# Second mixer of a two-block layer: gate tiles moved amid the last attention pairs, a sigmoid written as a tanh, and an output projection that starts with the state-space half

## The chip, the cores and the metric

The kernel runs on one core of a Trainium2 chip. The metric is the device time of one execution in microseconds (us); lower is better. The engines are PE (TensorE, the matrix engine, with a queue of weight loads of its own), DVE (VectorE), ACT (ScalarE), POOL (GpSimd) and SP (SyncE, which here only issues DMAs). Each runs its own instructions in order and waits on semaphores for the others.

## The reference, cut to what matters

Two blocks run one after the other on x of 512 tokens by 1024 features, all in float32. The change lies in the second block, between the end of its projections and its feed-forward network:

```python
def _s5(u, ...):                      # state-space half, 512 features
    ...                               # scan over time, y
    z = jax.nn.gelu(y.reshape(bsz, seq, D_SSM))
    out = z * jax.nn.sigmoid(z @ w_glu.astype(f32) + b_glu.astype(f32))
    return out.astype(u.dtype)

# second_block
y_ssm  = _s5(u, ...)
y_attn = _swa_sink(q, k, v, rel_bias, sinks[l])   # 8 heads, window of 128, sinks
mixed = jnp.concatenate([_rms(y_ssm, out_norm_ssm[l]),
                         _rms(y_attn, out_norm_attn[l])], axis=-1)
x = x + g1 * (mixed @ w_out[l])                   # 1024 x 1024
h2 = _rms(x, norm2_w[l]) * (1 + sc2) + sh2
x = x + g2 * _conv_ffn(h2, w_up[l], conv_w[l], conv_b[l], w_down[l])
```

## The kernel before

Activations lie transposed: features on the 128 partitions, the 512 tokens along the free axis, in tiles of 128 x 512. Every large product is made in three passes (`split_mm`, lines 133 to 135): weight and activation are each split in a rounded part and a rest, and hi·hi, hi·lo and lo·hi are added up in PSUM. Weights stream in chunks of 128 x 2048 through two buffers. For chunk n, SP loads it (`load_chunk`), ACT makes the rounded part (`round_chunk`, or `next_weights` inside the mixer), DVE the rest (`rest_chunk`, `next_rest`), and PE counts `w_used` up when it has used it, which lets ACT round chunk n + 1.

The second mixer is one block of code. After its projections comes a loop over 16 pairs, p = 0 to 15. A pair is two heads (r = 0, 1) and one chunk of 128 queries. For each pair

- PE makes `scores(p + 2)` and `turn(p)` (the transposes of the probabilities), and after every fourth pair `values(g)`;
- DVE makes `bias(p + 1)` (bias and maximum) and `normalise(p)`;
- ACT makes `exps(p)` and `move(p - 1)` (the transposed probabilities from PSUM to SBUF), and later `store(g)`.

So each pair goes PE, DVE, ACT, DVE, PE, ACT, with buffers for three pairs of probabilities and two banks of scores. Between the pairs, at places written out by hand, stands the rest of the state-space half: `lags(b)` and `from_states(b)` on PE, `output(b)` on ACT and `spin_back` on DVE:

```python
LAGS_AT, STATES_AT, OUTPUT_AT = (2, 5, 8), (3, 6, 10), (1, 4, 7, 11)
SPIN_AT = (1, 3, 5, 7, 9)
```

A second block of code follows when all engines have ended the first. ACT makes four GELUs and rounds them to `zhi`, DVE makes `zlo`, PE makes the gate product (48 matmuls of 128 x 512 into banks 0 to 3, feature by feature), ACT the sigmoid, DVE the product with z. Meanwhile the attention half is squared for its norm `r5`, rounded and split, and PE begins the output projection with it: `out2(c, ...)` is one half of one of four weight chunks, 24 matmuls. The order is attention 0, attention 1, state-space 0, state-space 1, and then attention and state-space in turn. Each norm's sum of squares goes through one float32 matmul with ones (`pe_sum`, line 194) after POOL has added up the squares. DVE scales each result by gate and root, POOL adds the attention part to x, and DVE the state-space part. Then comes the norm `r6` over x (`act_square`, `pe_sum` lines 194 and 197, `act_root`), a table load for SiLU (line 2674), `shifted_act` and `shifted_dve`, and the feed-forward network `ffn2`.

Of the kernel before, what the change touches and what calls it, by code (L numbers as in the profile page):

```python
# [166 lines left out]
class Norm:  # L167


    def __init__(self, k, name, acc, root, bank):  # L170
        self.acc, self.root, self.bank = acc, root, bank
        self.squared, self.added, self.summed, self.rooted, self.inverted, self.rounded, self.split = (
            k.sem(f"{name}_{what}") for what in
            ("squared", "added", "summed", "rooted", "inverted", "rounded", "split"))

    def act_square(self, act, k, src, j):
        if j >= 4:
            act.wait_ge(self.added, max(1, j - 4))
        act.activation(k.sq[:, j % 4, :], src, ACT.Square).then_inc(self.squared, 1)

    def add(self, eng, k, j):

        eng.wait_ge(self.squared, j + 1)
        if j == 1:
            ins = eng.tensor_tensor(self.acc[:, :], k.sq[:, 0, :], k.sq[:, 1, :], ALU.add)
        else:
            eng.wait_ge(self.added, j - 1)
            ins = eng.tensor_tensor(self.acc[:, :], self.acc[:, :], k.sq[:, j % 4, :], ALU.add)
        ins.then_inc(self.added, 1)

    def pe_sum(self, pe, k, added, tail):
# [3 lines left out]
        for j in tail:  # L195
            pe.wait_ge(self.squared, j + 1)
            mm = pe.matmul(self.bank[:, :], k.ones[:, :], k.sq[:, j % 4, :], start=False, stop=j == tail[-1])  # L197
# [425 lines left out]
def program(nc, io):  # L623
    root_ctx = ExitStack()
    with root_ctx:
# [724 lines left out]
        ssm_ctx = ExitStack()  # L1350
        powers = sb("b_powers", [P, TS, 2, 4, P], ctx=ssm_ctx)
# [496 lines left out]
        def _(pe):  # L1848
# [109 lines left out]
            for half in range(2):  # L1958
# [57 lines left out]
        root_a, root_b = k.root, square_sum  # L2016

# [12 lines left out]
        (sm_zhi, sm_zlo, sm_sig, sm_done, v_made, v_turned, v_summed, v_scanned, s_parts, s_made, lag_sum, lag_zero,  # L2030
         lag_set, lag_skip, y_made, y_sum) = (k.sem(f"ssm_{w}") for w in (
             "z_rounded", "z_split", "sigmoid", "done", "inputs", "turned_in", "summed", "scanned", "parts", "states",
# [14 lines left out]
        LAGS_AT, STATES_AT, OUTPUT_AT = (2, 5, 8), (3, 6, 10), (1, 4, 7, 11)  # L2047
        SPIN_AT = (1, 3, 5, 7, 9)
# [68 lines left out]
        def _(pool):  # L2117
            pool.wait_ge(lag_sum, 1)
            pool.memset(lag[:, :, :, :], 0.0).then_inc(lag_zero, 1)
            pool.wait_ge(h3_rounded, KT)  # L2120
            pool.wait_ge(h3_split, KT)
            pool.wait_ge(hot_in, 32)
            nc.clear_and_free_semaphores(feed_sems)

        @block.scalar
        def _(act):
# [95 lines left out]
            for p in range(PAIRS + 1):  # L2222
# [8 lines left out]
                if p == PAIRS - 1:  # L2231
                    act.preload_act_table_set("gelu_apprx_tanh_and_others")
# [4 lines left out]
                if p == 6:  # L2237
                    next_weights(OUT2)
                if p >= NT + 2 and p % NT == 2:
                    store(p // NT - 1)  # L2240
            store(3)
            own.act = chain.n

        @block.vector
        def _(dve):
# [73 lines left out]

            def bias(p):  # L2320
# [28 lines left out]
            chain.link(dve.tensor_scalar(g_heads2[:, 0:4], g_heads2[:, 0:4], HD ** -0.5, None, ALU.mult))  # L2349
            second_tile(IN2, 1)  # L2350
# [33 lines left out]
            for p in range(PAIRS):  # L2384
# [9 lines left out]
                if p == 2:  # L2394
                    next_rest(GLU)
                if p == 8:
                    next_rest(OUT2)
            own.dve = chain.n

        @block.tensor  # L2400
        def _(pe):
# [95 lines left out]

            pe.wait_ge(k.w_lo, IN2 + 1)
# [57 lines left out]
            for p in range(PAIRS):  # L2556
# [19 lines left out]
            values(NT - 1)  # L2576
        stage.close()
        gone(mix_ctx)
        gone(ssm_ctx)


        UP2 = OUT2 + 4
        tail_ctx = ExitStack()
        xhi = nc.alloc_sbuf_tensor_at("xhi_ffn2", [P, KT, S], R, offset=o_at)
        xlo = sb("xlo_ffn2", [P, KT, S], R, tail_ctx)
        hhi = sb("hhi2", [P, HALF, S], R, tail_ctx)
        hlo = sb("hlo2", [P, HALF, S], R, tail_ctx)
        zhi = sb("zhi", [P, 4, S], R, tail_ctx)
        zlo = sb("zlo", [P, 4, S], R, tail_ctx)
        part = sb("out2_part", [P, 4, S], ctx=tail_ctx)  # L2590
        root_a, root_b = sb("root_attn", [P, S], ctx=tail_ctx), sb("root_ssm", [P, S], ctx=tail_ctx)
        sum_b = sb("square_sum_ssm", [P, S], ctx=tail_ctx)
        r5 = Norm(k, "r5", square_sum, root_a, k.bank[6])
        r4 = Norm(k, "r4", sum_b, root_b, k.bank[7])
        r6 = Norm(k, "r6", square_sum, k.root, k.bank[6])
        h6_scaled, h6_rounded, h6_split = k.sem("norm2_scaled"), k.sem("norm2_rounded"), k.sem("norm2_split")
        out_a, part_a, part_b, added_a, added_b, stored = (
            k.sem(f"out2_{w}") for w in ("attn", "attn_scaled", "ssm_scaled", "attn_added", "added",
                                         "stored"))
        ffn2 = FeedForward(k, "ffn2", UP2, io["w_up2"], io["w_down2"], xhi, xlo, hhi, hlo)  # L2600
        o_attn, o_ssm = pr("o_attn"), pr("o_ssm")
        bank_a, bank_b = (4, 0, 6, 2), (2, 4, 0, 4)

        with nc.Block() as block:

            @block.sync
            def _(sp):
                for n in range(OUT2 + 3, ffn2.last):
# [329 lines left out]
```

## Time and profile before

| | us |
|---|---|
| median of 3 runs | 1252.51 |
| their range | 1252.3 to 1253.71 |
| the profiled execution's own time | 1248.42 |
| its span (first to last instruction) | 1246.3 |
| TensorE busy in the span | 1201.6 |
| VectorE busy | 772.5 |
| ScalarE busy | 486.8 |
| GpSimd busy | 62.1 |

The span is what the trace covers; the profiled execution was 2.1 us longer than that and 4.1 us shorter than the median of the runs. Busy time is summed over records; matmuls are pipelined, so a busy PE isn't one at its peak. The granted clock is given as a share of TensorE's 2.4 GHz, and a stretch at 0.50 ran at 1.2 GHz.

### The profile page before, as it was taken

The page shows a single profiled execution, that of the slowest core. Times are in us where ns is not written, and L with a number is a line of the kernel's source. Part 1 is how long each engine was busy: PE and PEld are TensorE (multiplying, and loading weights), DVE is VectorE, ACT ScalarE, POOL GpSimd, SP SyncE. Part 2 cuts the span into 40 slices and gives each one's busy share as a digit, 9 for nine tenths or more (in the row PEclk, how much of TensorE's full clock was granted, in tenths as well). Part 3 has the DMA queues.
Part 4 walks back from the last instruction along what each step waited for, and adds up shares of the span by engine and source line. Part 5 has one row for each costly group of instructions (what it writes and reads, how often), then busy time and mean ns, then how long its engine had stood idle before and what let it go on. Part 6 is the DMA issues. An engine that isn't in the chain of part 4 may idle for free. (4 is left out here: it accounts for less than half of the span.)

```text
span 1246.3 us, 14741 instructions
## 1 busy us (share of the span) xinstructions
PE 1201.6 (96%) x5909; PEld 938.9 (75%) x5909; DVE 772.5 (62%) x1274; ACT 486.8 (39%) x744; POOL 62.1 (5%) x76
## 2 busy tenths in 40 slices
PE   7999998899999999999998999789899999999998
PEld 5786666468778788878886885578688888888887
DVE  6537574756677777775876587656765543455542
ACT  6244545725322212222375234673444421343320
POOL 0000000013100000000022000034000000000000
PEclk9999999999999999999999999999999999999999
DMA  9312121223465576353226531102122223332222
GB/s 355 130 64 68 35 68 34 102 81 128 148 228 193 172 248 248 127 177 116 76 96 170 179 109 35 35 34 102 58 82 97 80 94 114 102 101 101 70 93 91
DMA packets 31884, 144.67 MB, mean 116 GB/s; under 512 B 3303, under 2 KB 9672, under 8 KB 22600
## 3 DMA queue, kind: packets, MB, share of 16 engines
q1 hardware_dynamic: 31816, 143.73, 33.9%
q8 instruction: 47, 0.77, 0.2%
q14 instruction: 21, 0.17, 0.0%
HBM read 136.90 MB, written 6.82 MB: 115 GB/s over the span
## 5 line engine op out<-in xcount | busy, mean ns | idle before, releaser
L133 PE MATMUL bank<-xhi_ffn,w_hi_part 128*128 128x512 f32 x704 | 278.2, 395 | 4.4 <-DVE xlo_ffn L233 4.4
L121 ACT ACTIVATE w_hi_part<-w_raw 128x2048 fp32r<-128x2048 f32 (+1 forms) x95 | 164.1, 1727 | 289.1 <-PE bank L135 287.3
L134 PE MATMUL bank<-xlo_ffn,w_hi_part 128*128 128x512 f32 x704 | 275.7, 392 | 0.0
L135 PE MATMUL bank<-xhi_ffn,w_lo_part 128*128 128x512 f32 x704 | 274.9, 391 | 0.0
L127 DVE TENSOR_TENSOR w_lo_part<-w_raw,w_hi_part 128x2048 fp32r<-128x2048 f32 (+1 forms) x95 | 195.4, 2057 | 94.5 <-ACT w_hi_part L121 91.3
L133 PEld LDWEIGHTS bank<-xhi_ffn,w_hi_part 128*128 128x128 f32 x704 | 132.6, 188 | 35.0 <-issue 6.6
L135 PEld LDWEIGHTS bank<-xhi_ffn,w_lo_part 128*128 128x128 f32 x704 | 132.6, 188 | 30.4
L134 PEld LDWEIGHTS bank<-xlo_ffn,w_hi_part 128*128 128x128 f32 x704 | 132.4, 188 | 28.5 <-issue 0.2
L361 DVE SCALAR_TENSOR_TENSOR squares<-bank,param,squares 128x511 f32<-128x511 f32 x88 | 63.9, 747 | 84.7 <-ACT squares L344 83.1
L133 PE MATMUL bank<-hhi,w_hi_part 128*128 128x512 f32 x240 | 94.6, 394 | 0.3 <-DVE w_lo_part L127 0.3
L133 PE MATMUL bank<-hhi_half,w_hi_part 128*128 128x512 f32 x240 | 94.1, 392 | 0.0
L134 PE MATMUL bank<-hlo,w_hi_part 128*128 128x512 f32 x240 | 93.5, 389 | 0.0
L134 PE MATMUL bank<-hlo_half,w_hi_part 128*128 128x512 f32 x240 | 93.4, 389 | 0.0
L135 PE MATMUL bank<-hhi,w_lo_part 128*128 128x512 f32 x240 | 93.4, 389 | 0.0
L135 PE MATMUL bank<-hhi_half,w_lo_part 128*128 128x512 f32 x240 | 93.4, 389 | 0.0
L448 DVE SCALAR_TENSOR_TENSOR mod_acc<-mod_w,mod_c,mod_acc 128x384 f32<-128x384 f32 x112 | 69.1, 617 | 10.1 <-DMA mod_w<-in_w_mod 6.8
L133 PE MATMUL bank<-xhi,w_hi_part 128*128 128x512 f32 x144 | 61.4, 426 | 7.2 <-DVE w_lo_part L981 7.2
L344 ACT ACTIVATE squares<-bank,param 128x512 f32<-128x512 f32 x44 | 31.9, 776 | 82.8 <-PE bank L135 82.8
L135 PE MATMUL bank<-xhi,w_lo_part 128*128 128x512 f32 x144 | 57.3, 398 | 0.0
L134 PE MATMUL bank<-xlo,w_hi_part 128*128 128x512 f32 x144 | 56.9, 395 | 0.0
L133 PEld LDWEIGHTS bank<-hhi_half,w_hi_part 128*128 128x128 f32 x240 | 45.0, 188 | 12.9 <-issue 2.9
L133 PEld LDWEIGHTS bank<-hhi,w_hi_part 128*128 128x128 f32 x240 | 45.0, 188 | 11.4 <-DVE w_lo_part L127 1.2
(359 smaller groups left out, 1789.8 us busy)
## 6 DMA issues: line engine op xcount, KB each, us to landing
mod_w<-in_w_mod SPq DMA_DIRECT2D x32, 768.0 KB, 4.4
w_raw<-in_w_gu SPq DMA_DIRECT2D x22, 1024.0 KB, 6.4
w_raw<-in_w_down SPq DMA_DIRECT2D x32, 704.0 KB, 4.2
w_raw<-in_w_up SPq DMA_DIRECT2D x22, 1024.0 KB, 4.9
w_raw<-in_w_in_f SPq DMA_DIRECT2D x8, 1024.0 KB, 4.9
w_raw<-in_w_out SPq DMA_DIRECT2D x8, 1024.0 KB, 4.9
w_raw<-in_w_in SPq DMA_DIRECT2D x5, 1024.0 KB, 4.9
x<-in_x SPq DMA_DIRECT2D x8, 256.0 KB, 6.0
```

Of the source, the lines that this page charges most:

```text
L121: act.activation(k.whi[:, slot, 0:width], k.raw[:, slot, 0:width], ACT.Copy).then_inc(k.w_hi, 1)
L127: dve.tensor_tensor(k.wlo[:, slot, 0:width], k.raw[:, slot, 0:width], k.whi[:, slot, 0:width].bitcast(F), ALU.subtract).then_inc(k.w_lo, 1)
L133: pe.matmul(out, whi, xhi, start=first, stop=False)
L134: pe.matmul(out, whi, xlo, start=False, stop=False)
L135: return pe.matmul(out, wlo, xhi, start=False, stop=last)
L344: act.activation(k.sq[:, s, :], k.bank[s][:, :], ACT.Identity, bias=bias[:, 2 * i + a:2 * i + a + 1], scale=taps[:, 6 * i + 3 * a + 2:6 * ...
L361: dve.scalar_tensor_tensor(out=y, in0=k.bank[s][:, 0:S - back], scalar=taps[:, tap:tap + 1], in1=y, op0=ALU.mult, op1=ALU.add).then_inc(se ...
L448: ins = dve.scalar_tensor_tensor(out=acc, in0=w, scalar=self.c[:, j:j + 1], in1=acc, op0=ALU.mult, op1=ALU.add)
```

## The change

What follows is one diff cut to its core; "..." marks what is left out.

- The second block of code is gone: its instructions follow in the first, so the engines don't meet between the two. The buffers are laid over tiles that are free by then.
- The state-space work moves to earlier pairs: the last `from_states` and `output` from pairs 10 and 11 to 7 and 8, the spins to pairs 0 to 4. The split of the gate's weights on DVE moves from pair 2 to pair 6.
- At pair 9 ACT loads the GELU table, makes four GELUs and loads the exp table. `zhi` and `zlo` are made at pairs 10 and 11.
- The gate product goes tile by tile, 12 matmuls each, all in bank 6: `glu(t)` stands ahead of `turn(12 + t)` and, from t = 1 on, waits for `gate_tanh(t - 1)` to have read the bank.
- sigmoid(a) is made as (1 + tanh(a/2))/2: tanh is in the exp table; the factor 1/2 goes into the bias, the gain and the squares; `gate(t)` is one DVE instruction that makes (tanh + 1)·z.
- Rounding, splitting and squaring of the attention half move to pairs 12 and 15 and behind the loop.
- The output projection goes state-space 0, attention 0, state-space 1, and so on in turn. POOL adds the state-space part, DVE the attention part.
- `pe_sum` of r4 and r5 takes two added tiles and one tail tile, which makes two float32 matmuls with ones where it was one.
- POOL clears the semaphores of an earlier block before the memset of the lag weights instead of after it, and DVE scales two small parameters by a half.

```diff
-        LAGS_AT, STATES_AT, OUTPUT_AT = (2, 5, 8), (3, 6, 10), (1, 4, 7, 11)
-        SPIN_AT = (1, 3, 5, 7, 9)
+        LAGS_AT, STATES_AT, OUTPUT_AT = (2, 4, 6), (3, 5, 7), (1, 4, 6, 8)
+        SPIN_AT = (0, 1, 2, 3, 4)
+        GELU_AT, GLU_AT = 9, 12
...
         @block.gpsimd
         def _(pool):
-            pool.wait_ge(lag_sum, 1)
-            pool.memset(lag[:, :, :, :], 0.0).then_inc(lag_zero, 1)
             pool.wait_ge(h3_rounded, KT)
             pool.wait_ge(h3_split, KT)
             pool.wait_ge(hot_in, 32)
+            pool.wait_ge(lag_sum, 1)
             nc.clear_and_free_semaphores(feed_sems)
+            pool.memset(lag[:, :, :, :], 0.0).then_inc(lag_zero, 1)
...
+            def attn_round(g):
+                act.wait_ge(l_stored, g + 1)
+                plain_round(act, r5, ahi[:, g, :], y[:, 4 + g, :], o_attn[:, g:g + 1])
+                r5.act_square(act, k, y[:, 4 + g, :], g)
+
+            def gate_tanh(t):
+                act.wait_ge(sm_made, t + 1)
+                act.activation(tanhs[:, t, :], k.bank[6][:, :], ACT.Tanh, bias=b_half[:, t:t + 1], scale=0.5)\
+                    .then_inc(sm_sig, 1)
+
+            def ssm_round(t):
+                act.wait_ge(sm_done, t + 1)
+                plain_round(act, r4, shi[:, t, :], y[:, t, :], o_half[:, t:t + 1])
...
-                if p == PAIRS - 1:
-                    act.preload_act_table_set("gelu_apprx_tanh_and_others")
                 if p >= 1:
...
-                if p == 6:
+                if p == 7:
...
+                if p == GELU_AT:
+                    act.preload_act_table_set("gelu_apprx_tanh_and_others")
+                    for t in range(4):
+                        act.wait_ge(y_sum, t + 1)
+                        act.activation(y[:, t, :], y[:, t, :], ACT.Gelu_apprx_tanh).then_inc(sm_gelu, 1)
+                    act.preload_act_table_set("exp_and_others")
+                if p in (GELU_AT + 1, GELU_AT + 2):
+                    for t in (0, 1) if p == GELU_AT + 1 else (2, 3):
+                        act.wait_ge(sm_gelu, t + 1)
+                        act.activation(zhi[:, t, :], y[:, t, :], ACT.Copy).then_inc(sm_zhi, 1)
+                if p == GELU_AT + 3:
+                    attn_round(0)
+                    attn_round(1)
+                if p == PAIRS - 1:
+                    attn_round(2)
+                if p > GLU_AT:
+                    gate_tanh(p - GLU_AT - 1)
+                if p > GLU_AT + 1:
+                    ssm_round(p - GLU_AT - 2)
+            ssm_round(3)
+            r4.act_square(act, k, y[:, 0, :], 0, 0.5)
+            r4.act_square(act, k, y[:, 1, :], 1, 0.5)
             store(3)
+            attn_round(3)
+            r4.act_square(act, k, y[:, 2, :], 2, 0.5)
+            r4.act_square(act, k, y[:, 3, :], 3, 0.5)
...
+            def gate(t):
+                dve.wait_ge(sm_sig, t + 1)
+                dve.scalar_tensor_tensor(out=y[:, t, :], in0=tanhs[:, t, :], scalar=1.0, in1=y[:, t, :], op0=ALU.add,
+                                         op1=ALU.mult).then_inc(sm_done, 1)
...
-                if p == 2:
+                if p == 6:
                     next_rest(GLU)
                 if p == 8:
                     next_rest(OUT2)
+                if p in (GELU_AT + 1, GELU_AT + 2):
+                    for t in (0, 1) if p == GELU_AT + 1 else (2, 3):
+                        split_z(t)
+                if p == GELU_AT + 3:
+                    attn_rest(0)
+                    attn_rest(1)
+                if p == PAIRS - 1:
+                    attn_rest(2)
+                if p > GLU_AT:
+                    gate(p - GLU_AT - 1)
+                if p > GLU_AT + 1:
+                    ssm_rest(p - GLU_AT - 2)
+            gate(3)
+            ssm_rest(2)
+            ssm_rest(3)
+            attn_rest(3)
...
+
+            def glu(t):
+                if t == 0:
+                    pe.wait_ge(k.w_lo, GLU + 1)
+                    pe.wait_ge(sm_zlo, 4)
+                else:
+                    pe.wait_ge(sm_sig, t)
...
+                for j in range(4):
+                    mm = split_mm(pe, k.bank[6][:, :], hi[:, j, P * t:P * t + P], lo[:, j, P * t:P * t + P],
+                                  zhi[:, j, :], zlo[:, j, :], j == 0, j == 3)
+                mm.then_inc(sm_made, 1)
+                if t == 3:
+                    pe.wait_ge(sm_made, 4)
+                    pe.sem_inc(k.w_used, 1)
...
+                if p >= GLU_AT:
+                    glu(p - GLU_AT)
...
+        bank_s, bank_a = (4, 2, 0, 4), (0, 4, 2, 0)
...
+            for j in (1, 2):
+                r5.add(pool, k, j)
+            r4.add(pool, k, 1)
+            r4.add(pool, k, 2)
+            for j in range(4):
+                add_ssm(j)
+            r6.add(pool, k, 1)
+            for j in (4, 5):
...
+        def _(act):
+            round_chunk(act, k, (OUT2 + 1) % 2, 16 * ((OUT2 + 1) // 2 + 1), OUT2)
+            act.preload_act_table_set("natural_log_exp_and_others")
+            r4.act_root(act, 4, eps_col[:, 0:1])
+            r5.act_root(act, 4, eps_col[:, 0:1])
+            round_chunk(act, k, (OUT2 + 2) % 2, 16 * ((OUT2 + 2) // 2 + 1), OUT2 + 1)
...
+            rest_chunk(dve, k, (OUT2 + 1) % 2, OUT2 + 2)
+            dve.wait_ge(r4.inverted, 1)
+            from_ssm(0)
+            dve.wait_ge(r5.inverted, 1)
+            from_attn(0)
+            from_ssm(1)
+            rest_chunk(dve, k, (OUT2 + 2) % 2, OUT2 + 3)
+            from_attn(1)
+            from_ssm(2)
+            rest_chunk(dve, k, (OUT2 + 3) % 2, OUT2 + 4)
+            from_attn(2)
+            from_ssm(3)
...
+            from_s(0)
+            r4.pe_sum(pe, k, 2, [3])
+            from_a(0)
+            r5.pe_sum(pe, k, 2, [3])
+            pe.wait_ge(l_stored, 4)
+            from_s(1)
+            pe.wait_ge(part_s, 2)
+            from_a(1)
+            pe.wait_ge(part_a, 2)
+            from_s(2)
+            pe.wait_ge(part_s, 4)
+            from_a(2)
+            pe.wait_ge(part_a, 4)
+            from_s(3)
+            pe.wait_ge(part_s, 6)
+            from_a(3)
+            pe.wait_ge(r4.rooted, 1)
+            r6.pe_sum(pe, k, KT - 5, list(range(KT - 4, KT)))
...
-                pe.wait_ge(k.w_lo, GLU + 1)
-                hi = k.whi[:, GLU % 2, :].rearrange("p (k n) -> p k n", n=S)
-                lo = k.wlo[:, GLU % 2, :].rearrange("p (k n) -> p k n", n=S)
-                for j in range(4):
-                    pe.wait_ge(sm_zlo, j + 1)
-                    for t in range(4):
-                        mm = split_mm(pe, k.bank[t][:, :], hi[:, j, P * t:P * t + P], lo[:, j, P * t:P * t + P],
-                                      zhi[:, j, :], zlo[:, j, :], j == 0, j == 3)
-                mm.then_inc(k.w_used, 1)
-                pe.wait_ge(r5.split, 4)
-                out2(0, bank_a[0], 4, out_a)
-                r5.pe_sum(pe, k, 3, [])
-                pe.wait_ge(sm_sig, 4)
-                out2(1, bank_a[1], 4, out_a)
-                pe.wait_ge(r4.split, 4)
-                out2(0, bank_b[0], 0, k.w_used)
-                r4.pe_sum(pe, k, 3, [])
...
```

## Rows read from the trace of the kernel before

**Rows 1.** The page's busy time, share of the span and instructions.
```profile
PE 1201.6 (96%) x5909; PEld 938.9 (75%) x5909; DVE 772.5 (62%) x1274; ACT 486.8 (39%) x744; POOL 62.1 (5%) x76
```

**Rows 2.** Windows by stage: bounds, length, busy time (instructions) of each engine, PE clock, DMA.
```profile
751.80:799.30 47.50, 40.91 (x433) 25.42 (x432) 36.59 (x134) 27.37 (x76) 0.00 (x0) 0.96 0.14 46
799.30:813.80 14.50, 7.77 (x51) 4.60 (x51) 4.81 (x21) 9.77 (x24) 0.00 (x0) 0.87 0.00 1
813.80:826.20 12.40, 12.40 (x48) 10.11 (x49) 6.69 (x7) 7.63 (x13) 4.14 (x3) 0.88 0.01 1
826.20:872.10 45.90, 45.90 (x198) 36.90 (x197) 30.21 (x33) 21.66 (x28) 21.30 (x14) 1.00 0.27 92
872.10:881.10 9.00, 4.46 (x11) 1.46 (x9) 7.07 (x9) 7.08 (x8) 0.25 (x1) 1.00 0.35 116
881.10:1246.30 365.20, 361.55 (x1584) 298.26 (x1584) 184.63 (x197) 119.42 (x130) 0.00 (x0) 1.00 0.27 90
```

**Rows 3.** The chain that ended last, about the projection and the norm behind it.
```profile
812.93 0.70 DVE zlo L2709
...
831.81 0.86 PE bank L194 x2
...
878.15 1.28 ACT L2674
```

**Rows 4.** Timeline of PE: start, length, line, operation, count, idle time before.
```profile
765.18 4.11 PE L2450 MATMUL bank<-proj,lag_weights 128*128 128x512 f32 x8
...
777.31 2.42 PE L2450 MATMUL bank<-proj,lag_weights 128*128 128x512 f32 x8
...
790.63 0.38 PE L2481 MATMUL bank<-kept,prob 128*128 128x128 f32 x2
...
793.99 1.94 PE L2459 MATMUL bank<-b_powers,c_lifted 128*32 128x127 f32 x64 [0.85 <-DVE b_powers L2307]
...
799.30 1.73 PE L2493 MATMUL bank<-probT,v 128*64 128x256 f32 x16 [0.93 <-ACT probT L2160]
...
805.65 0.66 PE L2481 MATMUL bank<-kept,prob 128*128 128x128 f32 x4 [1.07 <-DVE prob L2341]
807.20 3.10 PE L2493 MATMUL bank<-probT,v 128*64 128x256 f32 x16 [0.89 <-ACT probT L2160]
813.77 0.77 PE L133 MATMUL bank<-zhi,w_hi_part 128*128 128x512 f32 x1 [3.47 <-DVE zlo L2709]
...
825.53 0.39 PE L133 MATMUL bank<-zhi,w_hi_part 128*128 128x512 f32 x1
826.21 0.39 PE L133 MATMUL bank<-hhi,w_hi_part 128*128 128x512 f32 x1
```

**Rows 5.** Timeline of ACT, same columns.
```profile
803.66 0.51 ACT L2151 ACTIVATE prob<-prob,nmax 128x257 f32<-128x257 f32 x1
...
804.55 0.20 ACT L2151 ACTIVATION_READ_ACCUMULATOR prob<-prob,nmax 128x1 f32 x1
804.77 1.28 ACT L2232 ACT_TABLE_LOAD   x1
806.06 1.09 ACT L2160 ACTIVATE probT<-bank 128x512 f32<-128x512 f32 x2
...
816.81 2.20 ACT L179 ACTIVATE squares<-o_all 128x512 f32<-128x512 f32 x4
818.91 2.55 ACT L210 ACTIVATE hhi<-o_all,param 128x512 fp32r<-128x512 f32 x4
...
828.29 2.40 ACT L2652 ACTIVATE out_part<-bank,param 128x512 f32<-128x512 f32 x4
```

**Rows 6.** Timeline of DVE, same columns.
```profile
784.83 1.89 DVE L2301 TENSOR_TENSOR squares<-b_powers,cos_sin 128x512 f32<-128x512 f32 x3
```

**Rows 7.** Windows of 2.5 us about two falls of the PE clock, columns as in rows 2.
```profile
802.50:805.00 2.50, 0.78 (x6) 0.42 (x4) 1.49 (x10) 2.48 (x9) 0.00 (x0) 1.00 0.00 0
807.50:810.00 2.50, 2.50 (x14) 1.37 (x12) 0.00 (x0) 0.00 (x0) 0.00 (x0) 0.50 0.00 0
```

More of the change, by code:

```diff
@@ L196, in pe_sum @@
             pe.wait_ge(self.squared, j + 1)
-            mm = pe.matmul(self.bank[:, :], k.ones[:, :], k.sq[:, j % 4, :], start=False, stop=j == tail[-1])
+            mm = pe.matmul(self.bank[:, :], k.ones[:, :], self.sq[:, j % 4, :], start=False, stop=j == tail[-1])
         mm.then_inc(self.summed, 1)
@@ L2122, in _ @@
             pool.wait_ge(hot_in, 32)
+            pool.wait_ge(lag_sum, 1)
             nc.clear_and_free_semaphores(feed_sems)
+            pool.memset(lag[:, :, :, :], 0.0).then_inc(lag_zero, 1)
+        r5 = Norm(k, "r5", square_sum, root_attn, k.bank[7])
+        r4 = Norm(k, "r4", sum_b, root_ssm, k.bank[6], ssm_squares)
+        sm_gelu, sm_zhi, sm_zlo, sm_made, sm_sig, sm_done = (
+            k.sem(f"glu_{w}") for w in ("gelu", "z_rounded", "z_split", "made", "tanh", "done"))
         @block.scalar
@@ new lines, in program, with _ @@
+        ffn2 = FeedForward(k, "ffn2", UP2, io["w_up2"], io["w_down2"], xhi6, xlo6, hhi6, hlo6)
+        bank_s, bank_a = (4, 2, 0, 4), (0, 4, 2, 0)
+        @block.sync
+        def _(sp):
+            for n in range(OUT2 + 3, ffn2.last):
+                load_chunk(sp, k, n % 2, io["w_out2"][n - OUT2] if n < UP2 else ffn2.source(n), after_lo=n - 1)
+            for j in range(KT):
+                sp.wait_ge(ffn2.added, KT + j + 1)
+                sp.dma_start(io["out"][:, j, :], x[:, j, :]).then_inc(stored, 16)
+            sp.wait_ge(stored, 16 * KT)
@@ new lines, in _, with add_ssm @@
+        @block.gpsimd
+        def _(pool):
+            def add_ssm(j):
+                pool.wait_ge(part_s, j + 1)
+                pool.tensor_tensor(x[:, j, :], x[:, j, :], part[:, j % 2, :], ALU.add).then_inc(added_s, 1)
+            for j in (1, 2):
[6 more added lines that the diff above has]
+            for j in (4, 5):
+                add_ssm(j)
+            r6.add(pool, k, 2)
+            r6.add(pool, k, 3)
+            for j in (6, 7):
+                add_ssm(j)
@@ new lines, in _, with out2, from_s, from_a @@
+        @block.tensor
+        def _(pe):
+            def out2(c, bank, norm, his, los, first, done):
+                n = OUT2 + c
+                pe.wait_ge(k.w_lo, n + 1)
+                hi = k.whi[:, n % 2, :].rearrange("p (k n) -> p k n", n=256)
+                lo = k.wlo[:, n % 2, :].rearrange("p (k n) -> p k n", n=256)
+                for t in range(2):
+                    cols = slice(P * t, P * t + P)
+                    for j in range(4):
+                        if c == 0 and t == 0:
+                            pe.wait_ge(norm.split, j + 1)
+                        mm = split_mm(pe, k.bank[bank + t][:, :], hi[:, first + j, cols], lo[:, first + j, cols],
+                                      his[:, j, :], los[:, j, :], j == 0, j == 3)
+                return mm.then_inc(done, 1)
+            def from_s(c):
+                return out2(c, bank_s[c], r4, shi, slo, 0, out_s)
+            def from_a(c):
+                return out2(c, bank_a[c], r5, ahi, alo, 4, k.w_used)
+            from_s(0)
[16 more added lines that the diff above has]
+            r6.pe_sum(pe, k, KT - 5, list(range(KT - 4, KT)))
+            for half in range(2):
+                for i in range(HALF * half, HALF * half + HALF):
+                    ffn2.pe_up(pe, i, h6_split if i == 0 else None)
+                for j in range(KT):
+                    ffn2.pe_down(pe, half, j)
@@ L2579, in program @@
         gone(ssm_ctx)
[L2582 to L2591, printed above, removed]
@@ L2792, in program @@
-        gone(tail_ctx)
         gone(mid_ctx)
```

272 lines of the change are left out of this document (92 added, 180 removed).

## Prediction

> **What bounds the kernel now.** I read the page's busy times first: TensorE is busy for 96% of the span [rows 1], so time is to be won only where PE waits, works at the low clock, or repeats something. The windows by stage show where. The feed-forward network behind 881.1 us and the output projection from 826.2 to 872.1 are dense at full clock. The stretch that the change touches is not: from 751.8 to 826.2 the pairs, the hand-over and the gate product, with a mean clock of 0.96, 0.87 and 0.88 [rows 2]. Then I read PE's timeline there. The values of pairs 8 to 11 end at about 801.0 (799.30 and 1.7). From there to the first matmul of the projection at 826.21 [rows 4] pass 25.2 us. The reader is to see in these: the last transposes at 805.65; values at the low clock, 3.10 where the group before took 1.73; 3.47 us without a matmul, ended by zlo, after GELU and rounding; and a gate product of 12.44 us (813.77 to 826.21), where 48 matmuls at full clock take 10.9 (a group of three every 0.68, so 0.227 each) [rows 3, 4]. ACT and DVE are what to look at next, since the change puts some twenty ACT instructions and two table loads amid the pairs.
>
> **What is won at most.** The same work, from the end of that group of values, is now: four gate tiles of 12 matmuls, 2.72 each, 10.9; turns 12 to 15, 0.33 and three of 0.58, 2.1; the last values at full clock, 1.7. That is 14.7 without any wait. In the projection, each of the two norm sums is two float32 matmuls where it was one, 0.86 more each [rows 3], 1.7. PE's stretch of 25.2 thus becomes at least 16.4, and **8.8 us** are to be won. From them go D, how much later the first gate tile starts than 801.0, and W, all that PE waits or loses to the clock from there to the projection. The change of the time is D + W - 8.8.
>
> The rest: the barrier between the two blocks of code goes, inside the 25.2. The projection keeps its 192 matmuls and stays PE-bound; chunk OUT2 + 1 is rounded and split some 10 us behind the last move, where it is wanted 16 us behind it (values 1.7, two halves of 5.45, two sums of 1.7). 24 matmuls stand between a half and the next use of its bank, against 1.4 us of scaling on DVE. The end is the same: 9.0 us from the last matmul to the network, with the SiLU table load in it [rows 2, 3]. Two tiny DVE operations and POOL's clearing ahead of its memset come ahead of 751.8, beside the matmuls of the mixer's input projection, which hide them; I cost them at nothing, 0.5 if that cover were gone.
>
> **D, first part: the state-space work in front.** Up to turn(8) the changed order has one more `from_states` on PE, 1.94, one more set of spins on DVE, three operations of 0.6, 1.9 [rows 4, 6], and one more `output` on ACT, which I bound by two moves, 1.1 [rows 5]. DVE is the tight one here: a spin now stands ahead of bias(2) and normalise(1), and every pair up to 4 carries a set. Laying the queue entries one behind the other, with the start-to-start times of the rows and 0.16 us per hand-over, gives turn(8) 3.1 later than its 790.63. As a test the same laying-out of the old order, with the 1.7 us that one `lags` lost to the low clock (4.11 against 2.42 [rows 4]), puts turn(15) at 805.7; the trace has 805.65. The bounds are 0, if these fill waits, and 4.9, if all three add up.
>
> **D, second part: ACT at pairs 9 to 12.** Here ACT becomes the bound. In its queue between move(8) and values(2) stand: table load 1.28, four GELUs 2.1, table load 1.28, exps(10) 1.0, move(9) 0.5, store(1) 0.5, two roundings 1.0, exps(11) 1.0, move(10) 0.5, two roundings 1.0, exps(12) 0.8, move(11) 0.5; together 11.5. The prices are those of rows 5: a 128 x 512 ACTIVATE takes 0.52 (four squares in 2.20), a move every 0.5 (two in 1.09), a pair's two exps take 1.0, a load 1.28. With 0.8 from turn(8) to the first load, a hand-over and 1.7 of values, the first gate tile starts 14.0 behind turn(8). Before, the values ended 10.4 behind it. The difference is 3.7 (bounds 0, if ACT's old waits took all of it, and 6.7, all of the loads, GELUs and roundings). What is queued behind the loads is exps(10): normalise(10) and turn(10) wait for it, PE some 4 us. D is 3.1 + 3.7 = **6.8**.
>
> A table load costs 1.28 by the row: the exps end at 804.75, the load starts at 804.77 and the next move at 806.06 [rows 5]. The Trainium skill (ScalarE: Activation LUTs, What ACT_TABLE_LOAD costs) has 1.28 too, but adds a drain of 1.38 to each switch; by it the two switches at pair 9 would cost 2.8 us more than my sum. The trace shows no such drain.
>
> **W: one bank for four tiles.** All tiles are made in bank 6, so glu(t) waits for the tanh of the tile before, and ACT's queue puts move ahead of that tanh, which waits for turn. Tile, turn, hand-over, move, other ACT work, tanh, hand-over, tile: nothing of it overlaps. The tanh has no row; I take 0.6 of the sigmoid (2.40 for four, bias from a column [rows 5]); 0.52 of a plain ACTIVATE and 0.72 with its full latency are the bounds. Waits: 1.2 ahead of tile 1 (move 0.28, tanh 0.6, two hand-overs); 1.9 ahead of tile 2 (move 0.5, store(2) 0.5, tanh); 2.5 ahead of tile 3 (the rounding and square of attention tile 2, 1.14, stand ahead of the tanh); 1.0 ahead of the last values. Sum 6.6, bounds 5.5 and 8. The chain behind tile 3 (tanh 0.6, gate 0.7, rounding 0.62, rest 0.7, hand-overs) is about 3 us and lies beside values and nine matmuls, 3.7: it costs nothing, but 1 or 2 us if ACT is late there.
>
> The clock: before its fall at about 806 PE had been busy 0.78 of 2.5 us and ran transposes; then it was at 0.50 [rows 7]. Ahead of the first gate tile the schedule has the same picture, 9 us with transposes and scores and a 4 us hole. I therefore charge one spell at 1.2 GHz. The spells of the trace cost 1.4 (the values), 1.5 (the gate product) and 1.7 (the lags) [rows 4]; I take 1.6, with 0 and 2.7 (a whole tile at half speed) as bounds. The lags' spell in the front stays in both. W is 6.6 + 1.6 = **8.2**.
>
> **The sum.** 6.8 + 8.2 - 8.8 = +6.2 us. The profiled execution's own 1248.42 would be 1254.6; its distance to the median, 4.1, is kept: **1258.7**. This case's own range goes from D 3 and W 5.5 (-0.3) to D 9 and W 9.5 (+9.7), so 1252 to 1262.
>
> **The rivals.** A difference under 0.2% (2.5 us) is not to be told from no change.
>
> *ACT's work and the turnarounds are hidden.* ACT was busy 27.4 of 47.5 us of the pairs [rows 2] and has room; scores run two pairs ahead. If that slack took up the loads and GELUs, D would be 0 to 1, and if PE's queue covered half of the tile waits, W 3.3: D + W is 3.3 to 4.3, so about -5, 1247.5. It decides as soon as D + W is under 8.8, under 6.3 for a measurable gain. Against it: exps(10) cannot pass the loads, DVE and PE both need it, and each tile waits on one bank. 0.17.
>
> *The gain and the price cancel.* D 5 and W 4 to 6, the clock not falling: within 2.5 us, 1252.5. 0.18.
>
> *The clock stays low over the gate tiles.* The gaps between tiles are 2 to 3 us with only transposes in them, as before the fall at 806 [rows 7]. Then the first tile loses 1.1 more than charged and three lose 2.7 each, 9.3: 1268. Against it: to 799.3 the mean clock was 0.96 although PE's records cover only 40.9 of 47.5 us [rows 2], and a gate tile is denser work than transposes. 0.08. In a sentence beside it: the Trainium skill (TensorE: Matmul & The Clock Gate, Part 1) too ties the lower level to how busy PE has lately been.
>
> *The drain is real behind a GELU.* Were 2.8 us more lost at pair 9, as the page says, ACT would be later by as much and the time 1261.5. 0.03; the other load of rows 5 speaks against it.
>
> *The forecast*, slower by 2.5 to 10 us: 0.54.
>
> Slower holds 0.65, the same 0.18, faster 0.17. The range that leaves out most of the hidden case and the low clock, some 2 in 10, goes from 1249.5 to 1263.
>
> **What would show it.** Right: turn(8) about 794 instead of 790.6; two table loads and four GELUs on ACT at some 794 to 799 and a PE hole of 4 us behind turn(9); the first gate tile near 808; waits of 1 to 3 us ahead of each later tile, released by the tanh; the projection from about 831, 47.6 long with two float32 sums each time; the network at about 887 instead of 881.1, and 365 us from there as before. Wrong: a first gate tile before 804 (D), tiles back to back (W), gate tiles at 0.43 per matmul after the first (clock), or another length of projection or end.

## The result, and the profile after

The changed kernel is slower: 1262.74 us median of 4 runs (1260.09 to 1264.0) against 1252.4 (4 runs), ratio 1.0071 with a 95% interval of 1.0058 to 1.0083, so 7 to 10 us. Its profiled execution took 1260.09 us, 11.7 more than that of before (1248.42). The forecast was 1258.7, in a range up to 1263.0.

Windows by stage of the changed kernel. The columns are those of [rows 2]. The bounds are: turn(0), turn(8), the first gate tile, the first matmul of the output projection, the first of the norm r6 behind it, the first of the feed-forward network, the end.

```profile
760.89:796.43 35.54, 30.53 (x313) 19.22 (x313) 27.16 (x84) 17.68 (x46) 0.00 (x0) 0.86 0.10 31
796.43:811.87 15.44, 8.89 (x48) 5.00 (x47) 10.63 (x40) 14.96 (x36) 0.38 (x1) 0.67 0.19 68
811.87:835.23 23.36, 17.81 (x85) 12.90 (x83) 9.88 (x27) 10.79 (x26) 2.28 (x2) 0.93 0.00 1
835.23:883.08 47.85, 47.85 (x202) 37.70 (x201) 26.09 (x27) 18.63 (x23) 22.64 (x13) 1.00 0.19 67
883.08:892.34 9.26, 4.72 (x11) 1.65 (x10) 7.12 (x9) 7.07 (x8) 0.14 (x1) 1.00 0.63 221
892.34:1257.90 365.56, 361.61 (x1584) 298.32 (x1584) 184.69 (x197) 119.44 (x130) 0.00 (x0) 1.00 0.27 90
```

The reader is to see that the last row is nearly as long as that of before (365.20 in [rows 2]) and that the loss lies ahead of it. In the second row ACT is busy for 14.96 of 15.44 us, and PE has a clock of 0.67; in the first the clock is 0.86. In both kernels turn(0) starts within 0.4 us of the same time, and I count from there, since single executions differ ahead of the pairs: in the traces below turn(0) stands between 760.5 and 764.2. From turn(0) to the network are 131.45 us; the same stretch of the kernel before:

```profile
760.54:790.63 30.09, 26.67 (x249) 16.73 (x249) 25.98 (x82) 16.79 (x45) 0.00 (x0) 0.94 0.11 36
760.54:881.10 120.56, 103.68 (x648) 74.09 (x647) 82.18 (x184) 69.21 (x134) 25.70 (x17) 0.96 0.18 62
```

The difference is 10.9 us. It holds for these two executions; the traced one of before is a short one, as the run with two table loads shows below. PE's timeline of the changed kernel, with what answers to [rows 4] (the lags, the turns and values, the starts of the four gate tiles, the projection):

```profile
765.43 1.09 PE L2568 MATMUL bank<-kept,prob 128*128 128x128 f32 x4 [3.47 <-DVE prob L2410]
...
769.18 4.46 PE L2537 MATMUL bank<-proj,lag_weights 128*128 128x512 f32 x8
...
796.43 0.44 PE L2568 MATMUL bank<-kept,prob 128*128 128x128 f32 x2
798.77 0.66 PE L2568 MATMUL bank<-kept,prob 128*128 128x128 f32 x4 [1.27 <-DVE prob L2410]
804.10 1.11 PE L2568 MATMUL bank<-kept,prob 128*128 128x128 f32 x4 [4.25 <-DVE prob L2410]
...
809.60 2.34 PE L2580 MATMUL bank<-probT,v 128*64 128x256 f32 x16
811.87 0.49 PE L133 MATMUL bank<-zhi,w_hi_part 128*128 128x512 f32 x1
...
816.20 0.50 PE L133 MATMUL bank<-zhi,w_hi_part 128*128 128x512 f32 x1 [0.42 <-ACT glu_tanh L2192]
...
821.46 0.49 PE L133 MATMUL bank<-zhi,w_hi_part 128*128 128x512 f32 x1 [1.75 <-ACT glu_tanh L2192]
...
827.35 0.50 PE L133 MATMUL bank<-zhi,w_hi_part 128*128 128x512 f32 x1 [2.39 <-ACT glu_tanh L2192]
...
833.56 1.74 PE L2580 MATMUL bank<-probT,v 128*64 128x256 f32 x16 [0.69 <-ACT probT L2177]
835.23 0.50 PE L133 MATMUL bank<-ssm_hi,w_hi_part 128*128 128x512 f32 x1
```

Each tile after the first waits for the tanh of the one before. The hole of 4.25 us ahead of turn(10) ends with DVE's normalise; ACT's timeline shows what held that up:

```profile
796.90 0.38 ACT L2177 ACTIVATE probT<-bank 128x256 f32<-128x256 f32 x1 [0.34 <-PE bank L2568]
797.31 1.28 ACT L2271 ACT_TABLE_LOAD   x1
798.60 2.19 ACT L2274 ACTIVATE o_all<-o_all 128x512 f32<-128x512 f32 x4
800.80 1.28 ACT L2275 ACT_TABLE_LOAD   x1
802.10 0.51 ACT L2168 ACTIVATE prob<-prob,nmax 128x257 f32<-128x257 f32 x1
```

### The profile page after: what moved, and what is told of

Read it like the earlier page. It is cut to its first block, busy times and chain, and to the rows that moved or that the text cites. A ratio compares the mean times of both kernels' runs of the same rounds, so it can differ in the third digit from the quotient of the medians.

```text
span 1257.9 us, 14737 instructions
## 1 busy us (share of the span) xinstructions
PE 1207.9 (96%) x5913; PEld 942.0 (75%) x5913; DVE 771.7 (61%) x1276; ACT 486.7 (39%) x744; POOL 61.9 (5%) x74
## 4 chain that ended last, share of the span: by engine, by line
PE 76%; DVE 3%; ACT 3%; issue 1%; DVEq 0%; ACTq 0%
PE bank L133 23%; PE bank L134 23%; PE bank L135 23%; PE bank L2537 1%; PE bank L683 1%; PE bank L1865 1%; PE bank L2580 1%; PE bank L2505 1%; PE bank L2568 1%; DVE squares L362 0%; PE bank L198 0%; PE bank L2546 0%; DVE keep L1655 0%; PE bank L1858 0%; PE bank L2558 0%
## 5 line engine op out<-in xcount | busy, mean ns | idle before, releaser
L133 PE MATMUL bank<-hhi,w_hi_part 128*128 128x512 f32 x176 | 68.8, 391 | 0.3 <-DVE w_lo_part L127 0.3
L134 PE MATMUL bank<-hlo,w_hi_part 128*128 128x512 f32 x176 | 68.6, 390 | 0.0
L135 PE MATMUL bank<-hhi,w_lo_part 128*128 128x512 f32 x176 | 68.5, 389 | 0.0
L133 PEld LDWEIGHTS bank<-hhi_half,w_hi_part 128*128 128x128 f32 x240 | 45.1, 188 | 13.0 <-issue 2.9
L135 PEld LDWEIGHTS bank<-hhi_half,w_lo_part 128*128 128x128 f32 x240 | 45.1, 188 | 9.4
```

Of the source, the lines that this page charges most:

```text
L133: pe.matmul(out, whi, xhi, start=first, stop=False)
L134: pe.matmul(out, whi, xlo, start=False, stop=False)
L135: return pe.matmul(out, wlo, xhi, start=False, stop=last)
```

## The experiments

All but three start from the changed kernel. "From turn(0)" is each profiled execution's time from turn(0) to the network: 120.6 before, 131.5 changed. Ratios are to the kernel before, from executions made together with it.

**Gate tiles in three banks.**

```diff
-                else:
-                    pe.wait_ge(sm_sig, t)
+                elif t == 3:
+                    pe.wait_ge(sm_sig, 1)
+                else:
+                    pe.wait_ge(l_biased, 30)
...
-                    mm = split_mm(pe, k.bank[6][:, :], ...
+                    mm = split_mm(pe, k.bank[(6, 4, 5, 6)[t]][:, :], ...
...
+            pe.wait_ge(sm_sig, 3)
             from_s(0)
```

`gate_tanh(t)` reads the same bank. The last wait keeps the projection off a bank that a tanh has yet to read.

> The changed kernel, but gate tile 1 goes to bank 4 and tile 2 to bank 5 (the banks of the scores of pair 14, read by then), tile 3 to bank 6 again, so that no tile waits for the tanh just before it. Theory (W is the one bank): the waits of 0.4, 1.75 and 2.4 us ahead of tiles 1, 2 and 3 go, PE is dense and the spell at 1.2 GHz in tile 3 (about 1.7) goes with them; from the first tile to the projection 17 to 18 us instead of 23.4, the kernel 5 to 6 us faster than the changed one, ratio to the kernel before about 1.004. Rival (the tiles wait for ACT, whatever the bank, since turn and move hold them): the tiles move together but turn and values wait as long; the stretch stays at 22 or more, the time within 1.5 us of the changed kernel.

Ratio 1.0018 (1.0006 to 1.003), 124.7 us from turn(0). From the first tile to the projection:

```profile
811.80:828.48 16.68, 15.69 (x85) 11.70 (x83) 9.89 (x27) 10.80 (x26) 2.29 (x2) 1.00 0.01 1
```

23.36 us became 16.68, more than forecast, and the clock is 1.00. PE's records now fill 15.7 of 16.7 us. The one bank, with the clock that fell in its gaps, cost 6.7 us. With three banks the order of ACT's queue doesn't bind there.

**No table loads at pair 9.**

```diff
-                    act.preload_act_table_set("gelu_apprx_tanh_and_others")
...
-                        act.activation(y[:, t, :], y[:, t, :], ACT.Gelu_apprx_tanh)
+                        act.activation(y[:, t, :], y[:, t, :], ACT.Copy)
-                    act.preload_act_table_set("exp_and_others")
...
-                act.activation(tanhs[:, t, :], k.bank[6][:, :], ACT.Tanh, ...
+                act.activation(tanhs[:, t, :], k.bank[6][:, :], ACT.Identity, ...
```

> The changed kernel without the two table loads at pair 9; the four GELUs are plain copies and the tanhs an identity with bias and scale, so that no table is wanted (this leaves out the GELU and the nonlinearity of the gate; the ACTIVATEs stay in number, size and place). Theory (ACT's queue sets the time at pairs 9 to 12): exps(10) starts 2.6 us earlier, the PE hole ahead of turn(10) shrinks from 4.25 to 1.7, the first gate tile starts 2.6 us earlier or more (3 to 4) if the spell at 1.2 GHz goes too; the kernel 2.5 to 4 us faster. Rival (slack of the pairs hides the loads, D comes from the state-space work in front): the first tile no more than 1 us earlier. By the drain of 1.38 that the Trainium skill adds to a switch (ScalarE: Activation LUTs, What ACT_TABLE_LOAD costs) it would be 5.3 us earlier; that is a side bet, not part of the theory.

Ratio 1.0052 (1.0034 to 1.0069), 128.5 us from turn(0), 2.9 less. The same place of ACT's timeline:

```profile
797.60 0.38 ACT L2177 ACTIVATE probT<-bank 128x256 f32<-128x256 f32 x1 [0.33 <-PE bank L2566]
797.88 2.18 ACT L2273 ACTIVATE o_all<-o_all 128x512 f32<-128x512 f32 x4
799.96 0.50 ACT L2168 ACTIVATE prob<-prob,nmax 128x257 f32<-128x257 f32 x1
```

From move(8) to exps(10) 2.36 us instead of 5.20: two loads cost 2.84 with their seams, and turn(10) and turn(11) stand 2.8 us nearer to turn(8). The first tile stands 13.5 us behind turn(8) instead of 15.4, so 1.9 less; the rest of the gain was there eaten by the low clock, values taking 3.25 us instead of 2.34. The theory holds, with 1.9 where 2.6 or more was expected at the tile.

**One float32 matmul per norm sum.**

```diff
+            r5.add(pool, k, 3)
...
+            r4.add(pool, k, 3)
...
-            r4.pe_sum(pe, k, 2, [3])
             from_a(0)
-            r5.pe_sum(pe, k, 2, [3])
+            r4.pe_sum(pe, k, 3, [])
+            r5.pe_sum(pe, k, 3, [])
```

> The changed kernel, but POOL adds up all four tiles of squares of r4 and r5, each norm sum is one float32 matmul again, and both stand behind the first attention half. Theory: two float32 matmuls of 0.86 us less on PE, the projection 1.7 us shorter (46.1 instead of 47.8), the time 1.7 us less, which a ratio barely tells. Rival (DVE becomes late, since the root of r4 comes one half later): the projection as long or longer, a wait of some us ahead of the second attention half.

Ratio 1.0057 (1.0038 to 1.0076): by itself the run can't tell 1.7 us. The stage can: the projection took 46.15 us instead of 47.85, 1.7 less, without a new wait.

**Fillers to keep the clock up.** Fillers are matmuls whose results nobody reads.

```diff
                 if p == 1:
                     pe.wait_ge(h2_root, 2)
+                    pe.wait_ge(k.w_hi, GLU + 1)
+                    for _ in range(12):
+                        pe.matmul(k.bank[7][:, :], k.whi[:, GLU % 2, 0:P], k.whi[:, GLU % 2, 0:S], start=True, stop=True)
+                if p in (10, 11):
+                    pe.wait_ge(y_sum, 4)
+                    ... the same 12 into k.bank[6]
```

> The changed kernel with filler matmuls whose results nobody reads: 12 of 128 x 512 into bank 7 ahead of turn(1), and 12 into bank 6 ahead of turn(10) and of turn(11) each; 2.7 us each time at full clock, in holes of 3.5, 4.25 and 1.0 to 2 us. Theory (part of D is the low clock, 765 to 773 and 802 to 811 in the changed kernel): both spells go or shrink; scores, transposes, lags and values take their full-clock times, turn(8) comes 2 us earlier and the first gate tile 2 to 4 us earlier; the kernel 2 to 4 us faster although PE does 36 matmuls more. Rival (the clock costs nothing, DVE and ACT set the pace there): time as the changed kernel or up to 3 us slower by the fillers themselves.

Ratio 1.0022 (1.001 to 1.0034), 126.8 us from turn(0): 36 matmuls more, and 4.7 us less. turn(0) to turn(8), and turn(8) to the first tile:

```profile
760.77:792.50 31.73, 29.74 (x325) 19.66 (x325) 26.99 (x84) 18.06 (x46) 0.00 (x0) 1.00 0.10 35
792.50:807.25 14.75, 12.12 (x72) 8.15 (x70) 9.79 (x38) 13.97 (x33) 0.00 (x0) 1.00 0.20 71
```

35.54 became 31.73 and 15.44 became 14.75, both at a clock of 1.00. At full clock the first tile thus stands 46.5 from turn(0) instead of 51.0.

**The late spins one pair later.**

```diff
-        SPIN_AT = (0, 1, 2, 3, 4)
+        SPIN_AT = (1, 2, 3, 4, 5)
```

> The changed kernel with the five late sets of spins at pairs 1 to 5 instead of 0 to 4; all else as changed. Theory (the first part of D is the set of spins that stands ahead of bias(2) and normalise(1), and the low clock that the hole of 3.5 us ahead of turn(1) brings): turn(1) comes 2 us earlier, at about 763.2, the spell at 1.2 GHz is as short as in the kernel before, turn(8) comes 2 to 4 us earlier, and so does the first gate tile; the kernel 2 to 4 us faster than the changed one. Rival (the delay is PE's and ACT's added work up to pair 8, not the place of that one set): turn(1) earlier, turn(8) within 1 us of 796.4.

Ratio 1.0046 (1.0028 to 1.0063), 128.7 us from turn(0). turn(0) to turn(8) took 32.97 us instead of 35.54, 2.6 less. turn(1) came 1.9 us earlier, and the spell that the lags met ended sooner (3.82 instead of 4.46). The first gate tile came only 1.7 us nearer to turn(0), since the values ahead of it took 3.25 us instead of 2.34.

**Two table loads in the kernel before.**

```diff
+                if p == 9:
+                    act.preload_act_table_set("gelu_apprx_tanh_and_others")
+                    act.preload_act_table_set("natural_log_exp_and_others")
```

> The kernel before with two table loads added on ACT at pair 9, behind move(8), and nothing else. Theory (a load costs 1.28 us on ACT and only there; in the old order ACT has room at that place): turn(10) and turn(11) up to 1 us later, turn(15) 0 to 1 us later, the time within 1 us of the kernel before. Rival (loads stop the pairs in full, also in the old order): turn(15) and the time 2.6 us later, or 5.3 with the drain of 1.38 per switch that the Trainium skill states (ScalarE: Activation LUTs, What ACT_TABLE_LOAD costs).

Ratio 1.0015 (1.0001 to 1.0029), so 0.1 to 3.6 us. turn(15) stands 46.9 us from turn(0) instead of 45.1, but 1.4 of these 1.8 us are there at turn(8) already (31.5 instead of 30.1), ahead of the loads. From turn(8) on, turn(11) comes 0.9 later and turn(15) 0.4 (15.42 instead of 15.02). So the old order hides most of two loads, as the theory had it; the time alone can't tell, since its interval holds both the theory's 1 us and the rival's 2.6.

```profile
793.81 1.28 ACT L2236 ACT_TABLE_LOAD   x1
795.10 1.28 ACT L2237 ACT_TABLE_LOAD   x1
796.39 0.51 ACT L2151 ACTIVATE prob<-prob,nmax 128x257 f32<-128x257 f32 x1
```

Where the 1.4 us ahead of the loads come from, turn(1) shows, first before and then here, and the microsecond that lies 3.5 us behind turn(0), in the same order:

```profile
763.15 0.63 PE L2481 MATMUL bank<-kept,prob 128*128 128x128 f32 x4 [1.54 <-DVE prob L2341]
764.08 1.09 PE L2484 MATMUL bank<-kept,prob 128*128 128x128 f32 x4 [1.54 <-DVE prob L2344]
764.00:765.00 1.00, 1.00 (x6) 0.30 (x4) 1.00 (x3) 0.41 (x1) 0.00 (x0) 1.00 0.00 0
765.00:766.00 1.00, 1.00 (x6) 0.68 (x6) 1.00 (x3) 0.60 (x1) 0.00 (x0) 0.50 0.00 0
```

The work is the same up to here and the hole as long, 1.54 us. But the clock was down for some 3.5 us before (765.6 to 769) and for nearly 7 here (763.8 to 770.6). From turn(0) to the network this execution took 123.6 us; without the 0.4 of the loads that is 123.2, where the traced one of before took 120.6. Two executions of the old order thus differ by 2.6 us in this stretch. The low clock accounts for 1.4 ahead of turn(8), and behind turn(15) the gate product took 13.3 us instead of 12.4 at a clock of 0.81 instead of 0.88.

**The state-space work in front, alone.** An edit of the kernel before:

```diff
-        LAGS_AT, STATES_AT, OUTPUT_AT = (2, 5, 8), (3, 6, 10), (1, 4, 7, 11)
-        SPIN_AT = (1, 3, 5, 7, 9)
+        LAGS_AT, STATES_AT, OUTPUT_AT = (2, 4, 6), (3, 5, 7), (1, 4, 6, 8)
+        SPIN_AT = (0, 1, 2, 3, 4)
...
-                if p == 6:
+                if p == 7:
                     next_weights(OUT2)
...
-                if p == 2:
+                if p == 6:
                     next_rest(GLU)
```

> The kernel before with the new places of the state-space work alone: lags, from_states, output and spins in front as in the change, the splits of the gate and output weights moved with them; no GELU block, no gate tiles amid the pairs. Theory: turn(8) 3 to 6 us later as in the changed kernel, of which the pairs 9 to 15 give back about 1 to 3 since they hold less; the last values 2 to 4 us later, the kernel 2 to 4 us slower, ratio 1.0015 to 1.003. Rival (what is moved in front comes back in full behind): the last values within 1 us, ratio 1.000.

Ratio 1.0038 (1.0025 to 1.0052), about 5 us. turn(8) stands 35.4 from turn(0) as in the changed kernel, turn(15) 49.7 against 45.1, the network 126.5 against 120.6. Of the 5.3 us at turn(8), 0.7 came back up to turn(15). A good half of the loss needs no gate tile.

**Three mends together**: banks, one matmul per sum, fillers.

> The changed kernel with the three mends together: tiles 1 and 2 of the gate in banks 4 and 5, one float32 matmul per norm sum, and the filler matmuls ahead of turn(1), turn(10) and turn(11). Theory (they act on different terms and add up): first gate tile at about 807.2 as with the fillers alone, 16.7 us from there to the projection as with the banks, the projection 46.2 long, the network at 879.5; about 11 to 12 us faster than the changed kernel, ratio to the kernel before 0.999 (0.998 to 1.000). Rival (ACT's queue is the bound once PE waits no more on the bank): the stretch of the tiles grows back by 2 us or more when it starts earlier, ratio 1.001 or more.

Ratio 0.9962 (0.9948 to 0.9976), 1248.36 us: faster than both kernels. 118.5 us from turn(0), 13.0 less than the changed kernel; alone the mends gave 6.7, 1.7 and 4.7, together 13.1. They add up. The stretch came as forecast (118.7), the ratio lower than its 0.998 to 1.000. Against the 123.2 us above, 118.5 is 4.7 less, and the ratio says 4.8. First tile to projection, and the projection:

```profile
809.23:825.91 16.68, 15.69 (x85) 11.70 (x83) 10.83 (x28) 11.80 (x29) 2.67 (x2) 1.00 0.01 1
825.91:872.07 46.16, 46.16 (x199) 36.92 (x198) 27.72 (x27) 18.53 (x23) 25.27 (x15) 1.00 0.20 69
```

**The spins moved too**, on top of the three mends:

```diff
-        SPIN_AT = (0, 1, 2, 3, 4)
+        SPIN_AT = (1, 2, 3, 4, 5)
...
-                    for _ in range(12):
+                    for _ in range(6):
                         pe.matmul(k.bank[7][:, :], k.whi[:, GLU % 2, 0:P], k.whi[:, GLU % 2, 0:S], start=True, stop=True)
```

> The kernel with the three mends, and also the late spins at pairs 1 to 5, with 6 instead of 12 filler matmuls ahead of turn(1). Theory: with the clock kept up by the fillers, the place of the spins is worth only its own part of the hole ahead of turn(1): turn(8) stands 0.5 to 2 us nearer to turn(0) than the 31.7 us of the three mends, the time 0 to 2 us less. Rival (the place of the spins is worth the 2.6 us that it was alone, also with the clock kept up): turn(8) 2.6 us nearer or more.

Ratio 0.9955 (0.994 to 0.997), 1246.86 us. turn(0) to turn(8) 29.8 instead of 31.7: 1.9, at the upper end of the theory's 0.5 to 2.

**Fillers in the kernel before**, otherwise in its old order:

```diff
                 if p == 1:
                     pe.wait_ge(h2_root, 2)
+                    ... 6 fillers into k.bank[7]
+                if p in (14, 15):
+                    ... 5 fillers into k.bank[6]
                 turn(p)
...
+                for _ in range(14):
+                    pe.matmul(k.bank[7][:, :], k.whi[:, GLU % 2, 0:P], k.whi[:, GLU % 2, 0:S], start=True, stop=True)
                 pe.wait_ge(k.w_lo, GLU + 1)
```

> The kernel before with filler matmuls alone: 6 ahead of turn(1), 5 ahead of turn(14) and of turn(15) each, 14 ahead of the gate product. It asks whether what the three mends win over the kernel before is the clock alone, which the old order could have too. Theory: the old order loses 1.7 (lags), 1.4 (values) and 1.5 us (gate product) to the low clock; the fillers give back 3 to 4 of it, ratio 0.997 to 0.998, and the kernel with the three mends is level with it or 1 us ahead. Rival (the fillers cost PE as much as they bring): ratio 0.999 to 1.001, and the gain of the three mends belongs to the changed order.

Ratio 0.9954 (0.994 to 0.9968), 1247.65 us: 4 to 7.5 us less. More than forecast, and level with the mended change. turn(0) to turn(8), and to the network:

```profile
764.22:792.76 28.54, 26.53 (x255) 16.91 (x255) 25.73 (x82) 17.32 (x45) 0.00 (x0) 1.00 0.11 38
764.22:881.02 116.80, 106.07 (x677) 76.85 (x677) 81.93 (x184) 69.76 (x134) 25.68 (x17) 0.99 0.19 64
```

**zhi on DVE** instead of ACT, on top of the kernel with the spins moved:

```diff
-                        act.activation(zhi[:, t, :], y[:, t, :], ACT.Copy).then_inc(sm_zhi, 1)
...
             def split_z(t):
+                dve.wait_ge(sm_gelu, t + 1)
+                dve.tensor_copy(zhi[:, t, :], y[:, t, :]).then_inc(sm_zhi, 1)
                 dve.wait_ge(sm_zhi, t + 1)
```

> The kernel of the run before the last (three mends, spins at 1 to 5), and the four zhi are made by DVE copies instead of ACT's. Theory (ACT's queue sets D at pairs 9 to 12, DVE has room): four times 0.52 us leave ACT's queue between the loads and values(2), the first gate tile stands 1.5 to 2.1 us nearer to turn(8), the time 1.5 to 2 us less. Rival (DVE becomes the bound there, since it gets 1.4 to 2.5 us of copies): the first gate tile within 0.5 us.

Ratio 0.9956 (0.9939 to 0.9973). From turn(8) to the first tile 14.75 us, as without the edit. That doesn't bear the rival out: ACT's busy time there fell from 13.99 to 12.01 and DVE's rose only from 9.79 to 10.71 of 14.75, but 12 fillers ahead of turn(11) keep PE going from turn(10) on (turn(10) to turn(11) takes 4.12 us with them and 3.30 at the low clock without), so an earlier ACT changed nothing. The run says nothing on the theory.

**Banks and sums without fillers**, which completes a square.

> The kernel with the three mends without its filler matmuls: banks 4 and 5 for gate tiles 1 and 2, and one float32 matmul per norm sum. With the three mends it makes a square with the kernel before and the kernel before with fillers. Theory (the mends add up, and the fillers are worth as much in either order, 5 us): first gate tile at about 51 us from turn(0), 16.7 from there to the projection, the projection 46.2; the network 323 us... from turn(0) it stands about 123 us on, against 120.6 in the kernel before; ratio 1.000 to 1.002. Rival (the denser order keeps its clock up by itself): the network 121 us or less from turn(0), ratio 0.997 to 0.999.

Ratio 1.0003 (0.9994 to 1.0012), 123.1 us from turn(0). So:

| | without fillers | with fillers |
|---|---|---|
| kernel before | 1 | 0.9954 |
| change with banks and sums mended | 1.0003 | 0.9962 (0.9955 with the spins moved) |

## Why the prediction was right, and where it was off

The direction, the mechanisms and the places were right: D + W - 8.8 with D from the state-space work and ACT, W from the one bank. The sizes were too small. From turn(0), D measured 10.5 (5.5 up to turn(8) and 5.0 from there), W 8.7, and the projection grew by 2.2 instead of 1.7: 10.9 us for a forecast of 6.2. Two executions stood in for the kernels here, and that of before was short. Against the 123.2 us of the run with two loads the change costs 8.3 us, and by the ratio 8.9. The median of 1262.74 lies only 0.3 us inside the range; that is luck in part, for the profiled execution grew by 5.5 us more than forecast, and its distance to the median, kept at 4.1, turned out 2.65.

- **D, first part: 3.1 forecast, 5.5 measured.** The term was mis-sized by the clock. I had left the spell of the lags in both kernels as equal. In the change the hole ahead of turn(1) grew to 3.47 us, and the transposes, the spread and the lags behind it ran slow (1.09 and 4.46 us, against 4.11 for the lags in [rows 4]). With fillers in both orders, turn(0) to turn(8) is 31.7 changed and 28.5 before: 3.2, the laid-out 3.1. The queue work was priced right, its clock wasn't. Of the 2.4 us that were missing, 1.4 belong to the execution of before, whose clock was down for a shorter time than in the run with two loads; the rest came with the changed order.
- **D, second part: 3.7 forecast, 5.0 measured.** Again the order of ACT's queue was right, and the hole of 4 us stood where it was to stand. It turned values and two sets of transposes to 1.2 GHz. Without the low clock the stretch is 14.75 with the fillers, against 14.0 forecast. Removing the loads gave back 2.8 at turn(11) and 1.9 at the first tile; in the old order two loads cost 0.4 at turn(15). What the GELUs and the roundings cost of the rest is laid out and not tested.
- **W: 8.2 forecast, 8.7 measured.** The starts of the tiles are 4.33, 5.26 and 5.89 us apart, laid out as 4.25, 5.2 and 5.8. The floor beneath it was too low: a tile takes 2.90 us (811.87 to 814.77) instead of 2.72, and one set of scores (0.65) was left out; both are in the 16.7 us that the stretch still takes with three banks, where I had 14.7 without a wait. The one spell was charged to the first tile at 1.6; it fell into the last tile, which took 6.21 with turn and hand-over where 4.3 was laid out, and the first one had its share in D. The spell in the last tile follows the gaps of the one bank: with three banks there is none.
- **The rival of hidden work** failed on D + W, 19.2 against 8.8. **The clock staying low over the tiles** failed as put: three tiles ran at full clock. But its element, gaps with only transposes, did more than I charged, in the pairs. **The drain behind a table load** isn't there: the load ends at 802.08 and the exp starts at 802.10, and the two loads are worth 2.84 us. The Trainium skill (ScalarE: Activation LUTs, What ACT_TABLE_LOAD costs) would have 5.3 for them; the measurement decides.
- **The sums**: 1.7 forecast, 1.7 by the run that undoes them. The projection's other 0.5 lies in its matmuls: the last four halves of 24 start at 860.89, 866.51, 871.99 and 877.60, so those of the state-space part take 5.6 us and those of attention 5.5, where the first half before took 5.44. Why they are slower no run shows. The end, counted from the first matmul of the norm r6 (871.84 before, 883.08 after), is 9.26 in both, as forecast.

With banks and sums mended the time is that of before again (123.1 us from turn(0), against 123.2), although the state-space work in front, which cost about 5 us by itself, is still in it. From that I infer that the gate product amid the pairs gains a few us, but no run shows this alone. How the change would do with the state-space work at its old pairs wasn't tried: the GELUs want its last output at pair 9. The mended change with fillers beats the kernel before, but so does the kernel before with fillers, by as much; the rearrangement itself brings nothing that these runs can tell.

## What to carry to other kernels

Work moved into a latency-bound loop isn't free because its engine has idle time: lay out the queues of every engine through the loop, and look for the instruction that can't pass the newcomer (here the exps behind two table loads, and a tile behind the tanh of the tile before because of one bank). Give tiles that follow each other different PSUM banks as soon as any are free. And price a hole on PE not only by its length but by what runs slow behind it: a few matmuls that nobody reads, put into the holes, were worth 0.4 to 0.5% here in either order. Before you compare single traces, look whether the clock fell at the same place in both: here two executions of the same instructions stood 1.4 us apart by that alone.

## What the runs showed that I had not expected

Idle PE time of a few us, even with transposes in it, cost here twice: once as a wait, and once by the low clock behind it. Over the stretch from turn(0) to the network the mean clock was 0.96 before (0.91 in the run with two loads), 0.91 in the changed kernel, and 1.00 (118.5 us) with the three mends; 36 extra matmuls made the changed kernel 4.7 us faster in this stretch. In the kernel before, 30 fillers took 3.8 us off the traced 120.6, to 116.8 with a clock of 0.99, and 5.8 us off the time by the ratio. And the same instructions don't always meet the same clock: in two traces of the old order, with the same hole of 1.54 us, it fell 5.1 and 2.4 us behind turn(0), which moved turn(8) by 1.4 us.
